# A four-layer block on one core: the opening's modulation by single tiles, layer 0's scores in other banks

## The reference, cut to what matters

```
c_act = silu(c)                                     # c: 1 x 1024
mod = c_act @ ada_w[l] + ada_b[l]                   # 1024 -> 6144, once per layer
shift_m, scale_m, gate_m, shift_f, scale_f, gate_f = split(mod, 6)
h = rms_norm(x, g_pre_mix[l]) * (1.0 + scale_m) + shift_m
proj = h @ w_in[l] + b_in[l]                        # 1280 columns: q, k, v, u
q, k = partial_rotary(q), partial_rotary(k)
attn_out = softmax with a sink, window 128, 8 heads, 2 key heads
pool_out = (windowed mean - u) @ pool_w, four groups
mix = concat(attn_out, pool_out) @ w_out[l]
x = x + gate_m * rms_norm(mix, g_post_mix[l])
h = rms_norm(x, g_pre_ffn[l]) * (1.0 + scale_f) + shift_f
x = x + gate_f * rms_norm((silu(h @ w_gate) * (h @ w_up)) @ w_down, g_post_ffn[l])
```

## Time and profile before

| | us |
|---|---|
| median of 3 runs | 1170.52 (1170.49 to 1171.25) |
| the profiled execution | 1170.48 |
| its span, first to last instruction | 1168.5 |
| TensorE busy in the span | 1140.9 (98%) |
| VectorE, ScalarE busy | 811.5 (69%), 628.0 (54%) |
| moved by DMA | 254.04 MB, 217 GB/s over the span |

### The profile page before, as it was taken

How to read it: one execution, slowest core, us unless ns; L and a number is a source line. 1 busy time by engine, 2 the same in 40 slices (tenths; PEclk the granted TensorE clock), 3 DMA queues, 4 the chain that set the end, 5 groups by cost and what they waited for, 6 DMA issues and landing times.

```text
span 1168.5 us, 19588 instructions
## 1 busy us (share of the span) xinstructions
PE 1140.9 (98%) x7862; PEld 1020.5 (87%) x7862; DVE 811.5 (69%) x1258; ACT 628.0 (54%) x1113; POOL 29.0 (2%) x68
## 2 busy tenths in 40 slices
PE   7999999999999999999999999999999999999997
PEld 4556999999887999999899899999989889999996
DVE  6698988776998756645677667656656866766653
ACT  3077544445566544445666766445556676655443
POOL 3100000000000000000000000000000000000000
PEclk9999999999999999999999999999999999999999
DMA  9995998887445866556343546555534435555530
GB/s 361 413 378 220 355 365 329 319 334 268 189 164 198 319 231 225 210 190 238 128 181 109 180 174 217 180 183 183 187 139 156 145 132 195 196 186 194 181 109 37
DMA packets 37996, 254.04 MB, mean 217 GB/s; under 512 B 4537, under 2 KB 4881, under 8 KB 9874
## 3 DMA queue, kind: packets, MB, share of 16 engines
q1 hardware_dynamic: 35138, 243.95, 56.6%
q0 software_dynamic: 2624, 8.84, 2.1%
q10 hardware_dynamic: 144, 0.00, 0.0%
HBM read 251.69 MB, written 1.08 MB: 216 GB/s over the span
## 4 chain that ended last, share of the span: by engine, by line
PE 86%; DVE 6%; ACT 3%; DMA 3%; issue 1%; SPq 0%; DVEq 0%; ACTq 0%
PE bank L497 26%; PE bank L499 25%; PE bank L498 25%; PE bank L504 3%; DMA raw_w<-weights 2%; DVE raw_w L1641 2%; PE bank L546 2%; PE bank L595 2%; ACT gtok L1173 1%; DVE lo_w L1628 1%; DMA shared<-bias_rows 1%; PE bank L946 1%; DVE tok L1853 0%; PE bank L638 0%; PE bank L897 0%
## 5 line engine op out<-in xcount | busy, mean ns | idle before, releaser
L1628 DVE TENSOR_TENSOR lo_w<-raw_w,hi_w 128x1024 fp32r<-128x1024 f32 (+3 forms) x346 | 409.4, 1209 | 122.7 <-ACT hi_w L1168 122.3
L1168 ACT ACTIVATE hi_w<-raw_w 128x1024 fp32r<-128x1024 f32 (+3 forms) x346 | 350.6, 1040 | 103.9 <-PE bank L499 89.2
L497 PE MATMUL bank<-in_hi,lo_w 128*128 128x256 f32 x1408 | 396.0, 281 | 0.0
L499 PE MATMUL bank<-in_hi,hi_w 128*128 128x256 f32 x1408 | 392.8, 279 | 0.0
L498 PE MATMUL bank<-in_lo,hi_w 128*128 128x256 f32 x1408 | 392.8, 279 | 0.0
L497 PEld LDWEIGHTS bank<-in_hi,lo_w 128*128 128x128 f32 x1408 | 264.3, 188 | 2.6 <-issue 0.8
L498 PEld LDWEIGHTS bank<-in_lo,hi_w 128*128 128x128 f32 x1408 | 263.7, 187 | 1.9 <-issue 0.5
L499 PEld LDWEIGHTS bank<-in_hi,hi_w 128*128 128x128 f32 x1408 | 264.7, 188 | 0.0
L497 PE MATMUL bank<-hi_w,hid_lo 128*128 128x512 f32 x352 | 139.6, 396 | 0.2 <-DVE hid_lo L2116 0.2
L498 PE MATMUL bank<-lo_w,hid_hi 128*128 128x512 f32 x352 | 139.0, 395 | 0.0
L499 PE MATMUL bank<-hi_w,hid_hi 128*128 128x512 f32 x352 | 139.0, 395 | 0.0
(11 more groups left out here) (227 smaller groups left out, 1141.1 us busy)
## 6 DMA issues: line engine op xcount, KB each, us to landing
raw_w<-weights SPq DMA_DIRECT2D x213, 1024.0 KB, 4.9
ink<-ink_w SPq DMA_DIRECT2D x8, 640.0 KB, 13.9
rows<-mod_rows POOLq DMA_DIRECT2D x7, 512.0 KB, 6.9
rows<-norm_rows POOLq DMA_DIRECT2D x5, 512.0 KB, 4.9
raw_w<-weights SPq DMA_DIRECT2D x4, 512.0 KB, 8.9
ink<-whole_w SPq DMA_DIRECT2D x2, 1024.0 KB, 22.2
early_out<-whole_w SPq DMA_DIRECT2D x2, 1024.0 KB, 7.6
raw_w<-weights SPq DMA_DIRECT2D x2, 832.0 KB, 4.5
```

The source lines that it names most:

```text
L497: nc.tensor.matmul(o, st[1], mv[0], start=start, stop=False, **kw)
L499: return nc.tensor.matmul(o, st[0], mv[0], start=False, stop=stop, **kw)
L1168: nc.scalar.activation(hi_w[:, m % NSPLIT, cut], raw_view(unit)[:, cut], ACT.Identity).then_inc(*sig("hi_w", unit, i))
L1628: nc.vector.tensor_tensor(lo_w[:, m % NSPLIT, cut], raw_view(unit)[:, cut], hi_w[:, m % NSPLIT, cut].bitcast(F32), ALU.subtract).then_inc( ...
```

## The change

Loads: the vector table comes ahead of the first weights; the first eight units come as sixteen halves in the order of the tiles (two halves, then that tile's `ink` block). `INK_AFTER` goes. The bias load waits for ada(0,5) in place of ada(0,7). Silu is taken by ScalarE on the row before it is spread (table loaded first, and the other table after), and L1278 becomes a plain copy; the later silu table load, which serves the sine too, moves behind the copies of the turned tiles. VectorE scales one tile at a time; only the first half of each normed row is done ahead of it, the rest around tile 0, and its transposes on TensorE stand behind tile 0's products. The transposes of the vector table move ahead of those of the norm. So the bank of each job changes: `("in", 0, T, c)` hold 5, 6, 7, 0, 1, 2, the second transposes 3 and 4, and the score list becomes 5, 6, 7, 2, 3, 4. ada(0,8) moves from among the evacuations to behind `over_sum(0)`, and each later unit one place down. In ScalarE's list shares(3) and shares(4) stand before exps(4) and exps(5). The three parts of the constants share one semaphore name.

```diff
@@ -181,9 +181,6 @@
-INK_AFTER = {("ada", 0, 0): (1,), ("ada", 0, 1): (2,), ("ada", 0, 6): (3,), ("ada", 0, 2): (4,), ("ada", 0, 7): (5,),
-             ("ada", 0, 3): (6, 7)}
 WHOLE_AFTER = {("ada", 0, 9): 2, ("ada", 0, 10): 3, ("ada", 0, 17): 0, ("ada", 0, 19): 1}
@@ -711,6 +708,9 @@
                         done.then_inc(*sig("ink_used", kk))
+                        if kk == 0:
+                            for T in range(2):
+                                turn_norm(("mix", 0), T, (1,))
                     for T, c in places:
@@ -720,7 +720,7 @@
                         slice_of(7, T, c).then_inc(*sig("in", 0, T, c))
-                    banks(4, 5, 6, 7, 2, 3)
+                    banks(5, 6, 7, 2, 3, 4)
                     scores_late()
@@ -770,9 +770,9 @@
                         last.then_inc(*sig(*job))
-                pe.wait_ge(*due("const_mid", 0))
+                pe.wait_ge(*due("const_in", 1))
                 if L == 0:
-                    banks(0, 1, 4, 0, 1, *((6, 5, 7, 4) * 4))
+                    banks(0, 1, 5, 0, 1, *((7, 6, 5, 4) * 4))
                     pool_products()
@@ -985,15 +985,15 @@
             pe.wait_ge(*due("ve_step", 1))
-            pe.wait_ge(*due("c_in", 0))
+            pe.wait_ge(*due("c_act", "row"))
             for c in range(2):
...
             pe.wait_ge(*due("const_in", 0))
-            for T in range(2):
-                turn_norm(("mix", 0), T)
             pe.wait_ge(*due("vec_in", 0))
             transposes(("opening", "vec"), [vrow[:, P * g:P * (g + 1)] for g in range(NVEC)])
+            for T in range(2):
+                turn_norm(("mix", 0), T, (0,))
             for L in range(NL):
@@ -1010,34 +1010,43 @@
             sp.dma_start(const[:, 0:const_mid], a_const[:, 0:const_mid]).then_inc(*sig("const_in", 0, by=16))
-            at = [sum(kt * n_cols for _, kt, n_cols in UNITS[:n]) * P for n in range(3)]
-            tiles = [a_w[at[n]:at[n + 1]].rearrange("(p f w) -> p f w", p=P, f=2) for n in range(2)]
-            for n in range(2):
-                sp.dma_start(raw_w[:, n, 0:D], tiles[n][:, 0, :]).then_inc(*sig("ada_first", n, by=16))
             sp.dma_start(vrow[:, :], a_vec).then_inc(*sig("vec_in", 0, by=16))
-            sp.dma_start(ink[0], a_ink[0, :, :]).then_inc(*sig("ink_in0", by=16))
-            off = 0
+            size = 2 * D * P
+            def tiles_in(t, name):
+                j, f = t // 2, t % 2
+                for n in (2 * j, 2 * j + 1):
+                    if n >= NRAW and f == 0:
+                        sp.wait_ge(*due("ada", UNITS[n - NRAW][0]))
+                    src = a_w[size * n:size * (n + 1)].rearrange("(p f w) -> p f w", p=P, f=2)[:, f, :]
+                    sp.dma_start(raw_w[:, n % NRAW, D * f:D * (f + 1)], src).then_inc(*sig(name(n), t, n, by=16))
+            for t in range(KT):
+                tiles_in(t, (lambda n: f"tile_in{t // 2 % 2}") if t % 2 == 0 else (lambda n: f"raw_w{n % NRAW}"))
+                sp.dma_start(ink[t], a_ink[t, :, :]).then_inc(*sig(f"ink_in{t}", by=16))
+            off = size * KT
             for n, (unit, kt, n_cols) in enumerate(UNITS):
+                if n < KT:
+                    continue
                 if unit == ("ada", 0, 9):
-                    sp.dma_start(const[:, const_mid:const_late], a_const[:, const_mid:const_late]).then_inc(*sig("const_mid", 0, by=16))
+                    sp.dma_start(const[:, const_mid:const_late], a_const[:, const_mid:const_late]).then_inc(*sig("const_in", 1, by=16))
                 if unit == ("gu", 1, 8):
...
                     sp.wait_ge(*due("poolw", 1, 1))
-                    sp.dma_start(const[:, const_mid:], a_const[:, const_late:]).then_inc(*sig("const_late", 0, by=16))
+                    sp.dma_start(const[:, const_mid:], a_const[:, const_late:]).then_inc(*sig("const_in", 2, by=16))
                 if n >= NRAW:
...
                     sp.wait_ge(*due(*(("ada", old) if old[0] == "ada" else ("lo_w", old, 1))))
-                part, src = ((raw_w[:, n, D:2 * D], tiles[n][:, 1, :]) if n < 2 else
-                             (raw_view(unit), a_w[off:off + P * kt * n_cols].rearrange("(p w) -> p w", p=P)))
-                sp.dma_start(part, src).then_inc(*sig(f"raw_w{n % NRAW}", unit, by=16))
+                sp.dma_start(raw_view(unit), a_w[off:off + P * kt * n_cols].rearrange("(p w) -> p w", p=P)).then_inc(
+                    *sig(f"raw_w{n % NRAW}", unit, by=16))
                 off += P * kt * n_cols
...
                     sp.dma_start(whole[u].rearrange("p t c -> p (t c)"), a_whole[u, :, :]).then_inc(*sig(f"whole_in{u}", by=16))
-                for kk in INK_AFTER.get(unit, ()):
-                    sp.dma_start(ink[kk], a_ink[kk, :, :]).then_inc(*sig(f"ink_in{kk}", by=16))
             for T in range(2):
@@ -1109,8 +1118,9 @@
             angles()
+            pool.wait_ge(*due("ada", ("ada", 0, 5)))
+            load(bias, a_bias[0:1, :], 1280, "bias_in", 0)
             pool.wait_ge(*due("ada", ("ada", 0, 7)))
-            load(bias, a_bias[0:1, :], 1280, "bias_in", 0)
             pool.dma_start(sinks[:, :, :], a_sinks.rearrange("(o l) n -> o l n", o=1).to_broadcast([P, 2, HEADS])).then_inc(*sig("sinks_in", 0, by=16))
@@ -1147,6 +1157,10 @@
             sc.dma_start(pos_i[:, :], a_pos).then_inc(*sig("pos_in", 0, by=16))
+            sc.preload_act_table_set("silu_and_others")
+            sc.wait_ge(*due("c_in", 0))
+            nc.scalar.activation(c_row[0:1, :], c_row[0:1, :], ACT.Silu).then_inc(*sig("c_act", "row"))
             sc.preload_act_table_set("natural_log_exp_and_others")
@@ -1271,14 +1285,14 @@
                 nc.scalar.activation(r, r, ACT.Exp, scale=-0.5).then_inc(*sig("rstd", N, 1))
-                sc.preload_act_table_set("silu_and_others")
                 sc.wait_ge(*due("opening", "c", 1))
                 for c in range(2):
-                    nc.scalar.activation(c_row[:, cols(c)], ps(("opening", "c", c))[:, :], ACT.Silu).then_inc(*sig("c_act", c, frees=("opening", "c", c)))
+                    copy(("opening", "c", c), c_row[:, cols(c)], ps(("opening", "c", c))[:, :], "c_act", c)
                 for c in range(2):
...
                         copy(("tr", N, T, c), raw[:, 4 * c:4 * c + 4, P * T:P * (T + 1)], by_tile(ps(("tr", N, T, c))), "turned", T, c)
+                sc.preload_act_table_set("silu_and_others")
                 sc.wait_ge(*due("turns", 1))
@@ -1347,11 +1361,11 @@
                     probT_in(0)
+                    shares(3)
                     exps(4)
-                    shares(3)
                     probT_in(1)
+                    shares(4)
                     exps(5)
-                    shares(4)
                     probT_in(2)
@@ -1631,15 +1645,20 @@
                 unit = ("ada", l, n)
+                no = UNIT_NO[unit]
                 if f == 0:
                     in_turn(unit)
-                if f == 0 and UNIT_NO[unit] < 2:
-                    ve.wait_ge(*due("ada_first", 1))
-                elif f == 0 or UNIT_NO[unit] < 2:
-                    ve.wait_ge(*due(f"raw_w{UNIT_NO[unit] % NRAW}", unit))
+                if no >= KT:
+                    if f == 0:
+                        ve.wait_ge(*due(f"raw_w{no % NRAW}", unit))
+                elif f == 0:
+                    ve.wait_ge(*due(f"tile_in{no // 2 % 2}", no // 2 * 2, no // 2 * 2 + 1))
+                else:
+                    ve.wait_ge(*due(f"raw_w{no % NRAW}", no // 2 * 2 + 1, no))
                 w = raw_view(unit).rearrange("p (f k) -> p f k", f=2)[:, f, :]
                 ins = nc.vector.scalar_tensor_tensor(w, w, 1.0, c_row[:, :], ALU.mult, ALU.mult, accum_out=mods[:, l, 2 * n + f:2 * n + f + 1])
-                return ins.then_inc(*sig(*(("ada", unit) if f == 1 else ("ada_first", unit))))
+                return ins.then_inc(*sig("ada", unit)) if f == 1 else ins
             def ada(l, n):
@@ -1702,11 +1721,11 @@
                     nc.vector.tensor_tensor(scaled[:, cols(c)], x[:, T, cols(c)], rows[:, 1, cols(c)], ALU.mult).then_inc(*sig("scaled", N, T, c))
-            def norm(N, T):
+            def norm(N, T, parts=(0, 1)):
                 ve.wait_ge(*due("rstd", N, 1 if N == ("mix", 0) else T))
                 r = tok_rstd[:, T, 1:2]
-                for c in range(2):
+                for c in parts:
                     dst = final[:, T, cols(c)] if N[0] == "final" else normed[:, cols(c)]
@@ -1813,34 +1832,29 @@
                 for T in range(2):
-                    norm(N, T)
-                ve.wait_ge(*due("c_act", 1))
-                ada_tile(0, 4, 0)
-                ada_tile(0, 0, 0)
+                    norm(N, T, (0,))
                 ve.wait_ge(*due("opening", "vec"))
                 nc.vector.tensor_copy(vcol[:, :], ps(("opening", "vec"))[:, 0:NVEC * P]).then_inc(*sig("vcol", 0, frees=("opening", "vec")))
+                ve.wait_ge(*due("c_act", 1))
                 scale, shift = (modcol[:, ROWS[(0, kind, 0)], :] for kind in ("scale", "shift"))
```

(49 more changed lines are left out.)

## The result

The changed kernel takes 1172.75 us (median of 20 runs, 1171.82 to 1174.52), the kernel before 1170.97 (20 runs, 1170.05 to 1172.1): a ratio of 1.0017, 95% interval 1.0011 to 1.0023. It is slower by 1.8 us, real and still inside the 0.2% that the prediction took as the least that can be told from no change. The forecast of 1170.1 was wrong, and the time lies above the range's end of 1172.0. The profiled execution spans 1170.9 us against 1168.5.

What follows compares the result with a forecast made beforehand. Bound: TensorE (98% busy) and, nearly level at 102 us, gu(0,0)'s landing through an almost always full load queue. Ffn-norm transposes 0.68 us less, landing 0.35 later: about -0.4 from 1170.52, so 1170.1; range 1168.1 to 1172.0.

Steps and rivals of the forecast that it cites:

- What takes it back: After layer 0's scores: scale column at 81.9, TensorE 2.5 us ahead at most; ada(0,17) lands 0 to 0.7 late, gu(0,0) 93.3.
- Tile by tile: Opening's products: 4.3 us per tile, stall before tile 2 gone, first product ends at 44.2, gain 0.3 us.
- Rival B: The queue of loads runs dry at ada(0,16) and ada(0,17); gu(0,0) lands at 94.7, time 1171.5; chance 0.24.
- Bias: Layer 0's first evacuation no longer waits for its bias load, issued earlier, and starts at 44.3: -2.0 us.
- Scores follow at once: Layer 0's scores, in freed banks, start at 52.7 instead of 55.67; first softmax step at 53.94, -2.97 us.
- The 1.41 goes: Fourth block's probabilities ready at 68 instead of 74.14, so TensorE's 1.41 us stall before them disappears.
- Opening's front: Start of the kernel: silu on one row costs nothing, c ready at 9.1, TensorE starts at 14.9 against 14.71 (+0.2).
- table loads: ScalarE's two early table loads around silu fit while it is idle, with no drain added; costed at nothing.
- the wait of TensorE before the norm: New TensorE wait of about 2 us before the transposes of layer 0's ffn norm, behind gu(0,0)'s landing.
- rival C: gu(0,0)'s landing depends on issue and chance; without 1.5 us it lands at 91.5, time 1168.0 (-2.5); chance 0.14.

Runs made afterwards that it cites:

- banks and shares: Kernel before with only layer 0's scores in other banks and the shares ahead of the exponents: 1169.0 us, ratio 0.9982.
- opening alone: Kernel before with only tile-by-tile modulation, silu on one row and the new order of the opening's loads: 1175.28 us, ratio 1.0032 (five executions).
- all but the opening: Kernel before with the bias load two units earlier, other banks, shares ahead and ada(0,8) one place later: 1171.64 us, ratio 1.0007.
- one load fewer: Changed kernel with the 1 MB load of ada(0,15) left out, its shift columns made from old data: 1172.54 us, ratio 1.0009.

## Why the prediction was wrong

**The step that failed: "What takes it back", both halves, and before it "Tile by tile".** The forecast let the softmax start at 53.94 and so the late ada(0,8) cost 0 to 0.7 us of landing. It started at 56.11, 2.17 late; ada(0,16) and ada(0,17) were issued at 61.22 and 64.90 in place of 59.0 and 62.7, exactly that 2.2 later; gu(0,0) landed at 94.97 in place of 93.3. On VectorE's side the scale column came at 83.95 in place of 81.9, so TensorE was not 2.5 us ahead of the kernel before but level with it. Rival B described this mechanism and gave a landing of 94.7, +1.0 and 1171.5; at 0.24 it had too small a chance, and its price was small too: for 94.97 the mark moved 1.48, the medians 1.8.

Two relations that hold from run to run, each between two rows of one profile, show how it is paid (the last column is TensorE's wait for the normed rows before its transposes):

| kernel | first softmax step | scale column | difference | gu(0,0) lands | mark | difference | TensorE waits |
|---|---|---|---|---|---|---|---|
| before | 56.91 | 82.45 | 25.54 | 92.95 | 115.74 | 22.8 | none |
| banks and shares | 55.28 | 80.80 | 25.52 | 90.97 | 113.22 | 22.25 | 0.25 |
| changed, ada(0,8) back | 55.93 | 81.49 | 25.56 | 92.41 | 114.67 | 22.3 | 1.01 |
| opening alone | 60.98 | 86.52 | 25.54 | 97.04 | 119.82 | 22.8 | none |
| late ada(0,8) alone | 56.05 | 83.89 | 27.84 | 94.82 | 117.08 | 22.3 | 1.01 |
| all but the opening | 55.20 | 83.03 | 27.83 | 93.99 | 116.24 | 22.25 | 1.04 |
| changed | 56.11 | 83.95 | 27.84 | 94.97 | 117.22 | 22.25 | 1.10 |

From the first softmax step to the scale column VectorE is all but full: 25.54 us, and 27.84 with one unit more. The forecast had counted this one (2.3 us) and was right in it. What it lacked was the start. And where the landing ends last, the mark stands 22.3 behind it; before, TensorE's own work ended 0.5 later than that, as the prediction had it (0.68). So the late ada(0,8) is paid on two paths at once: against the kernel with it back in place the scale column comes 2.46 later and the landing 2.56 later. The landing ends last, by the 1.10 that TensorE waits; filling the queue alone would have given back no more than that.

**Tile by tile.** Forecast: a tile 4.3 us, tile 1 ended at 24.8, last scale ready at 43.3, first product ended at 44.2. Measured: tile 0 took 7.4, the last scale ended at 45.07, the first evacuation began at 47.08. There are two errors. The last scale was 1.8 late, since the bias now stands ahead of the tiles' loads in full: with the opening alone, whose bias load comes later, that scale ended at 43.45, close to the forecast. The forecast hung it on the last `ink` load (43.15; it landed at 44.24), for which a scale doesn't wait; it waits for the weights, and from the last such wait, at 38.60, VectorE worked without a gap to 45.07. And the idle time before tile 0 had grown from 1.74 to 4.89, since the transposes that used to fill it had been moved behind the tile; I costed their move as +1.3 and left out what their absence does to the passes that follow. In the changed kernel TensorE runs from tile 0 to the end of its passes without a wait, so there the slow tile decides, 47.08 for the first evacuation; with tile 0 fast the late scale decides, and it comes at 46.28. Of the 2.8 us by which 44.3 was missed, the first error by itself gives 2.0.

**Bias.** Forecast -2.0; measured +0.7 for the first evacuation in the whole change and -0.6 on the kernel before. The wait was taken away, but I had said that the load takes the queue's time either way and costed that at nothing; it is the 1.15 us by which TensorE's passes ended later above. I also missed that the new order of the opening moves ada(0,7), which the load waited for; the change names another unit there, and without that the opening cost 4.1 us at the mark.

**Banks and shares.** "Scores follow at once": right, they have no wait. On the kernel before that and the shares are worth 1.6 us at the softmax and 2.0 at the landing, more than the whole change was thought to bring. "The 1.41 goes": right for the whole change, where TensorE waits 2.27 for VectorE's column a little later instead. With the shares alone a wait of 1.53 us for VectorE stood in its place.

**Opening's front, table loads, the wait of TensorE before the norm:** right in kind. c was ready at 8.9 (forecast 9.1), the new wait was 1.10 and not 2. The spread of the scale row waited 2.27 for VectorE and began at 84.17, not 81.9.

**The prediction's rival C.** It hoped for 1.5 us from the gap of 4.0 us ahead of gu(0,0)'s landing. The gap did shrink, to 2.3, but the load ahead of it landed 3.7 later.

The change thus has parts with opposite signs. Taken in this order, at the mark: opening with its bias repair, the banks and the shares, -1.07; late ada(0,8) on top of them, +2.55. In another order the shares of the parts come out otherwise, as its price of 1.3 on the kernel before shows.

## What to carry to other kernels

A product whose end frees a load's buffer is part of the load queue: before moving it later, count the loads in flight at the moment when its issue will come, from the worst start of the work ahead of it and not from the forecast one. Where a wait names a unit of work as its time mark (the bias load here), an edit that reorders the units moves the wait too. And work that fills a gap ahead of an engine's run may be worth more where it stands than the time it takes: here its absence cost tile 0 2.9 us, of which at most 0.8 reached the end.

## What the runs showed of the hardware

Groups of TensorE in 15.5 to 22 us of the changed kernel, then in 26 to 40 (line, shapes, count, busy us, mean ns of one, idle before):
```profile
L702 PE MATMUL bank<-ink,raw 128*128 128x512 f32 x7 | 5.5, 923 | 4.9 <-DVE raw L1855 4.9
L702 PE MATMUL bank<-ink,raw 128*128 128x256 f32 x4 | 1.9, 634 | 0.0
...
L702 PE MATMUL bank<-ink,raw 128*128 128x512 f32 x27 | 12.2, 592 | 0.0
L702 PE MATMUL bank<-ink,raw 128*128 128x256 f32 x14 | 3.7, 379 | 0.0
```
The same kind of pass (512 columns) took 923 ns on average behind 4.89 us of idleness and 592 later, while the granted clock of that stretch reads 1.00:
```profile
16.00:18.00 2.00, 2.00 (x3) 0.67 (x2) 1.99 (x4) 0.00 (x0) 1.92 (x2) 1.00 1.04 423
```
With twenty matmuls in that gap it was gone. The length of the gap alone doesn't tell: the first 24 passes took 10.45 us behind 1.76 us of idleness in the kernel with the late ada(0,8) alone, and 8.83 behind 2.02 in the one with banks and shares, where their program is the same. Elsewhere the column did fall with the passes (0.75 in the kernel with the opening alone, whose TensorE had waited 2.50 and 0.99 us; 0.72 behind 2.27 us in the kernel with one load fewer), and in the changed kernel 2.27 us of the same waiting did nothing. So the durations of the passes are what to read; the column is right when it falls and not always when it stays. The Trainium skill, "TensorE: Matmul & The Clock Gate", section "Seeing it yourself", warns that the clock's trace events on trn2 have been unreliable and should be checked against another measure; this trace agrees.
